# Prompt attention's value products for two heads at a time, with the linear states' load behind that stage

## What is computed

```python
s = q @ k.T - slope * dist            # 8 heads: 2 groups g of 4 heads r, head size 64
p = softmax(where(dist >= 0, s, -inf))
o_branch = p @ v                      # branch 1: selected, branch 2: window
o_a = gate[0] * o_cmp + gate[1] * o_slc + gate[2] * o_win
```

## Time and profile before

| | |
|---|---|
| median of 3 runs | 2163.66 us (2163.35 to 2164.55) |
| profiled execution | 2164.54 us, its span in the trace 2162.8 us |
| TensorE, VectorE, ScalarE, GpSimd busy | 2110.7, 1173.1, 517.1, 648.7 us |
| attention stage of the prompt, first layer | about 306 to 459 us of the span |
| granted TensorE clock, mean | 0.992 of full |

### The profile page before, as it was taken

How to read it: one execution, slowest core, us unless ns; L and a number is a source line. 1 busy time by engine, 2 the same in 40 slices (tenths; PEclk the granted TensorE clock), 3 DMA queues, 4 the chain that set the end, 5 groups by cost and what they waited for, 6 DMA issues and landing times.

```text
span 2162.8 us, 30298 instructions
## 1 busy us (share of the span) xinstructions
PE 2110.7 (98%) x11911; PEld 1689.1 (78%) x11911; DVE 1173.1 (54%) x2384; ACT 517.1 (24%) x1108; POOL 648.7 (30%) x617
## 2 busy tenths in 40 slices
PE   8998989999999999999999989899999999999999
PEld 7787866678888888888887867666788888888887
DVE  5566667855346555453336666687554364555522
ACT  3124124542112222210112231244321222222000
POOL 4240041103323444434331300421132234444332
PEclk9999999999999999999999999999999999999999
DMA  5874541112222222322283736211132222223222
GB/s 149 273 238 173 217 152 40 40 42 100 78 82 78 78 78 79 98 74 79 67 289 118 267 133 252 80 40 40 42 120 82 78 78 78 78 81 95 79 71 75
DMA packets 172303, 237.52 MB, mean 110 GB/s; under 512 B 39551, under 2 KB 151680, under 8 KB 169408
## 3 DMA queue, kind: packets, MB, share of 16 engines
q1 hardware_dynamic: 153320, 133.11, 20.4%
q0 software_dynamic: 18400, 102.36, 12.8%
q10 hardware_dynamic: 444, 0.12, 0.0%
HBM read 222.76 MB, written 21.11 MB: 113 GB/s over the span
## 4 chain that ended last, share of the span: by engine, by line
PE 91%; DVE 4%; ACT 2%; DMA 2%; issue 1%; POOL 0%; DVEq 0%; SPq 0%; ACTq 0%; POOLq 0%
PE PS L981 52%; PE PS L924 10%; PE PS L1139 6%; PE PS L946 5%; PE PS L972 3%; PE PS L1474 2%; PE PS L1391 2%; PE PS L460 2%; PE PS L1402 2%; DMA arena<-in_cache_kv_slc_dram,idx 2%; ACT arena L1685 1%; PE PS L1349 1%; DVE arena L2398 1%; PE PS L1374 1%; PE PS L1523 1%
## 5 line engine op out<-in xcount | busy, mean ns | idle before, releaser
L981 PE MATMUL PS<-arena,ring 128*128 128x272 f32 x1632 | 401.3, 393 | 0.9 <-DVE xT L2051 0.6
L981 PEld LDWEIGHTS PS<-arena,ring 128*128 128x128 f32 x1632 | 309.3, 190 | 66.0 <-issue 2.4
L1685 ACT ACTIVATE arena<-PS 128x272 f32<-128x272 f32 (+12 forms) x442 | 176.5, 423 | 723.7 <-PE PS L981 286.0
L2051 DVE TENSOR_TENSOR arena<-PS,arena 128x272 f32<-128x272 f32 (+4 forms) x298 | 138.7, 476 | 353.4 <-PE PS L981 263.4
L981 PE MATMUL PS<-hT,ring 128*128 128x272 f32 x1120 | 283.4, 398 | 5.9 <-DVE arena L2051 4.8
L981 PEld LDWEIGHTS PS<-hT,ring 128*128 128x128 f32 x1120 | 214.2, 193 | 53.6 <-DVE arena L2051 5.2
L2051 DVE TENSOR_TENSOR xT<-PS,xT 128x272 f32<-128x272 f32 x224 | 98.9, 442 | 252.2 <-PE PS L981 252.0
L840 POOL TENSOR_TENSOR qT<-ring 128x512 f32<-128x512 f32 (+1 forms) x38 | 48.8, 1285 | 385.5 <-PE PS L981 255.4
L2057 DVE SCALAR_TENSOR_TENSOR arena<-arena,prm 128x32 f32<-128x32 f32 (+1 forms) x176 | 144.1, 819 | 22.2 <-ACT arena L1685 18.2
L924 PE MATMUL PS<-hT,ring 128*128 128x272 f32 x640 | 153.9, 401 | 0.8 <-DVE small L2521 0.8
L981 PE MATMUL PS<-arena,kv_kT 128*128 128x272 f32 x616 | 149.7, 392 | 0.0
(11 more groups left out here) (361 smaller groups left out, 2975.1 us busy)
## 6 DMA issues: line engine op xcount, KB each, us to landing
ring<-in_w_up_dram SPq DMA_DIRECT2D x88, 512.0 KB, 4.6
ring<-in_w_in_dram SPq DMA_DIRECT2D x68, 512.0 KB, 4.8
ring<-in_w_down_dram SPq DMA_DIRECT2D x32, 512.0 KB, 4.4
arena<-in_state_kv_win_dram POOLq DMA_DIRECT2D x4, 2048.0 KB, 9.0
ring<-in_w_out_dram SPq DMA_DIRECT2D x16, 512.0 KB, 4.5
out_dram<-in_state_kv_win_dram POOLq DMA_DIRECT2D x2, 4064.0 KB, 39.7
ring<-in_w_down_dram SPq DMA_DIRECT2D x16, 384.0 KB, 3.5
ring<-in_w_in_dram SPq DMA_DIRECT2D x16, 256.0 KB, 4.6
```

The source lines that it names most:

```text
L981: mm = pe.matmul(PS[:, bank, 0:HALF], weight[:, k, :], rhs(k), start=(start and k == 0), stop=(stop and k == kc - 1), skip_group_check=not ...
L1685: return nc.scalar.activation(out, in_, func, **kw)
L2051: return nc.vector.tensor_tensor(out, a, b_, op)
```

## The change

Units are taken in another order: for a query tile, heads 0 and 1 with branch 1, then heads 0 and 1 with branch 2, then heads 2 and 3. Two successive units 2p and 2p+1 then have the same keys and values. Their probabilities go side by side into one buffer PTp[p % 2] of two units (key tile, unit, query), and values(p) makes one product of 256 moving columns for each key tile and group, on every even step, ahead of that step's filler. pv counts pairs. block_values moves to the first even step behind. The second buffer of PTp takes the place of S0, so GpSimd's load of S0 moves behind all the SIDED weight sums and waits for the last pv.

```diff
@@ -366,7 +366,7 @@
         kcp = sb("kcp", 32)
         vcp = sb("vcp", P)
         ex = [carve(1024 * i, 2, SEQ) for i in range(3)] + [carve(6144, 2, SEQ)]
-        PTp = [carve(3072 + 1024 * i, 2, SEQ) for i in range(2)]
+        PTp = [carve(off, 2, QT, 2, P) for off in (3072, 19136)]
 
         rT = carve(10048, GH, NT)
         xrows = xT[:, :, :].rearrange("p k n -> p (k n)")
@@ -450,15 +450,16 @@
             b = S.banks(act, f"on{h}")
             run(two(rsg[h]), pair2(b), ACT.Sqrt, bias=eps_c, scale=float(D_MODEL // DV)).then_inc(*S.drain(act, f"on{h}"))
 
-        def values(pe, units, j):
-
-            qt, r, br = units[j]
-            for g in range(G):
-                pe.wait_ge(*S.drained(pe, f"e{j}{g}"))
+        def values(pe, units, p):
+
+            qt, r, br = units[2 * p]
+            for j in (2 * p, 2 * p + 1):
+                for g in range(G):
+                    pe.wait_ge(*S.drained(pe, f"e{j}{g}"))
             for t in range(qt + 1):
                 for g in range(G):
-                    mm = pe.matmul(PS[HD * g:HD * g + HD, VBANKS[qt % 2], P * r:P * r + P], kv[:, t, 1 + br, P + HD * g:P + HD * g + HD],
-                                   PTp[j % 2][:, g, P * t:P * t + P], start=False, stop=(r == R - 1 and br == 1 and t == qt))
+                    mm = pe.matmul(PS[HD * g:HD * g + HD, VBANKS[qt % 2], P * r:P * r + 2 * P], kv[:, t, 1 + br, P + HD * g:P + HD * g + HD],
+                                   PTp[p % 2][:, g, t, :, :].rearrange("p u n -> p (u n)"), start=False, stop=(r + 1 == R - 1 and br == 1 and t == qt))
             mm.then_inc(*S.inc(pe, "pv"))
 
         def w_slot_free(eng, name):
@@ -825,8 +826,6 @@
 
                 gp.wait_ge(*S.at(gp, "arena_gla"))
                 gp.nop().then_inc(*S.inc(gp, "settled"))
-                for b in range(NB):
-                    gp.dma_start(S0[:, b, :, :], ins["state_gla"][one, b].rearrange("o (a c) k v -> (o c k) a v", c=2)).then_inc(*S.inc(gp, "s0_in", 16))
                 def weight_sums(name):
 
                     n, s = SEVEN_AT[name], wslot(name)[0]
@@ -857,6 +856,10 @@
                 gp.tensor_tensor(low[:, :, HALF:NT], high[:, :, HALF:NT], low[:, :, HALF:NT], ALU.subtract).then_inc(*S.inc(gp, "g_sum"))
                 for name in SIDED[1:]:
                     weight_sums(name)
+                gp.wait_ge(*S.at(gp, "pv"))
+                gp.nop().then_inc(*S.inc(gp, "settled"))
+                for b in range(NB):
+                    gp.dma_start(S0[:, b, :, :], ins["state_gla"][one, b].rearrange("o (a c) k v -> (o c k) a v", c=2)).then_inc(*S.inc(gp, "s0_in", 16))
                 gp.wait_ge(*S.at(gp, "gla_states", 1))
                 gp.nop().then_inc(*S.inc(gp, "settled"))
                 gp.dma_start(o_gla_p[one].rearrange("o q (a c) k v -> (o q c k) a v", c=2), states[:, 8, :, :]).then_inc(*S.inc(gp, "state_stored", 16))
@@ -1381,7 +1384,7 @@
                         mm = pe.matmul(PS[bb:bb + 32, b, 0:P], ptn[0:NS, bb:bb + 32], kv[0:NS, 4, 1, P:2 * P], start=False, stop=True)
                     mm.then_inc(*S.fill(pe, f"os{hf}"))
 
-                units = [(qt, r, br) for qt in range(QT) for r in range(R) for br in range(2)]
+                units = [(qt, r, br) for qt in range(QT) for r0 in (0, 2) for br in range(2) for r in (r0, r0 + 1)]
 
                 def score(j):
                     qt, r, br = units[j]
@@ -1438,13 +1441,14 @@
                     if j + 3 < len(units):
                         score(j + 3)
                     turn(j)
-                    if (j - 1) % (2 * R) == 0:
-                        block_values((j - 1) // (2 * R))
-                    values(pe, units, j - 1)
+                    if j % 2 == 0:
+                        if (j - 2) % (2 * R) == 0:
+                            block_values((j - 2) // (2 * R))
+                        values(pe, units, j // 2 - 1)
                     side(("u", j), "S")
                     if j in GATE_UP_AT:
                         gate_up(GATE_UP_AT[j])
-                values(pe, units, len(units) - 1)
+                values(pe, units, len(units) // 2 - 1)
                 pe.wait_ge(*S.at(pe, "kd_ready", 1))
                 pe.wait_ge(*S.claim(pe, "S", "kd"))
                 b = S.banks(pe, "kd")
@@ -1906,12 +1910,12 @@
                         exps(done)
                         done += 1
                     w = P * (qt + 1)
-                    if j >= 2:
-                        act.wait_ge(*S.at(act, "pv", j - 1))
+                    if j >= 4:
+                        act.wait_ge(*S.at(act, "pv", j // 2 - 1))
                     for g in range(G):
                         act.wait_ge(*S.filled(act, f"e{j}{g}"))
                         b = S.banks(act, f"e{j}{g}")
-                        run(PTp[j % 2][:, g, 0:w], PS[:, b, 0:w], ACT.Copy).then_inc(*S.drain(act, f"e{j}{g}"))
+                        run(PTp[j // 2 % 2][:, g, 0:qt + 1, j % 2, :], PS[:, b, 0:w].rearrange("p (t n) -> p t n", n=P), ACT.Copy).then_inc(*S.drain(act, f"e{j}{g}"))
                     decay_step(DECAY_EXP_AT.get(j))
 
 
@@ -2581,7 +2585,7 @@
 
                 def attended(qt):
 
-                    dv.wait_ge(*S.at(dv, "pv", 2 * R * (qt + 1)))
+                    dv.wait_ge(*S.at(dv, "pv", R * (qt + 1)))
                     copy(AT[:, :, P * qt:P * qt + P], PS[:, VBANKS[qt % 2], :].rearrange("p (r n) -> p r n", r=R)).then_inc(*S.inc(dv, "at_out"))
 
                 def decay_step(step):
```

## The result

The kernel after takes 2175.70 us (median of 4 runs, 2174.38 to 2176.45), the one before 2163.51 beside it (4 runs, 2162.60 to 2164.55): ratio 1.0056, 95% interval 1.0038 to 1.0073. The forecast was 2165.6, in a range to 2169.0: the direction (slower, by some 2 us) was right, and the size was missed by 10 us. The profiled execution took 2174.38 us, its span is 2172.6 (before 2162.8), TensorE busy for 2113.2 us (before 2110.7).

What follows compares the result with a forecast made beforehand. TensorE, busy for 98% of the span, was taken as the bound. First layer -0.3 + 1.5 and second -0.3 + 1.0 gave +1.9 us on the median of 2163.66: 2165.6 us, range 2158.5 to 2169.0.

Steps and rivals of the forecast that it cites:

- Part 1: Attention stage without its first three steps: merged value products gain 2.6 us a layer, 0.3 after returned waits.
- steps 3, 7, 12, 29 and 31: Attention-loop steps where TensorE loses part of the merging gain: 0.37, 0.2, 0.16, 0.4 and 1.0 us a layer.
- The lower bound of the gain: Merged value products, before returned waits: at least 2.4 us a layer, around an expected 2.6.
- Part 2: GpSimd's S0 load, eight issues of 5.86 us, moves behind the last values product: costs nothing.
- Part 3: GpSimd's earlier sums lock VectorE in weigh(0) and weigh(1), delaying turn(0) and first filler: 1.5 us lost first layer, 1.0 second.
- Rival A: VectorE's first instructions get through before GpSimd's sums, turn(0) stays: up to -2.4 us a layer, 2158.8 to 2162; chance 0.22.
- ends near 324.9 instead of 323.4: 1.5 us lost: First filler's end in the first layer's attention stage, with TensorE's full clock back at 321.7: 1.5 us later.
- rival B: Half clock around the first units lasts one step longer: +1.7 us in one or both layers, 2167.3 to 2169.0; chance 0.18.

Runs made afterwards that it cites:

- The hold: Kernel after with one more wait: GpSimd holds its first sum until VectorE has finished weigh(0) and weigh(1); 2156.89 us, 0.9976 of before.
- The hold until weigh(2): Kernel after with block_values back in step 1 and GpSimd's sums held until weigh(2) is done; 2166.87 us, 1.0018 of before.
- the second repetition of the kernel after: Kernel after, unchanged, run again beside three other kernels on one chip; 2172.52 us, 1.0039 of before.
- the split: Kernel after with one group of the side product between the second and third of the four sampled updates; 2170.77 us, 1.0034 of before.
- the delay experiment: Kernel after with the eight transposes of kd done three times, ahead of the mixers; 2186.05 us, 1.0043 of before.

## Why the prediction failed, point by point

- **Part 1.** Right in its terms: 0.43 us a merged tile, waits of 0.22, 0.22, 0.35, 0.40 and 0.89 us at steps 3, 7, 12, 29 and 31 (forecast 0.37, 0.2, 0.16, 0.4 and, with the group's saving, 1.0). The stage behind its first steps gained 1.15 us a layer instead of 0.3. By group, from the second layer, with full clock there in both profiles: values 2.6 us less, waits 2.1 more, and 0.65 less on turns and fillers, which follow one another closer where no value product stands between them (with one key tile, turn to filler 0.28 instead of 0.37 us). That last term the sum lacks, and it is most of the difference between 0.3 and 1.15. (The lower bound of the gain was mis-added: 16 x 0.15 + 40 x 0.44 = 20.0, so 2.2 and not 2.4.)
- **Part 2.** Right: eight issues in 5.86 us behind the last product, no wait at the reader. Beside VectorE's copies and memsets an issue took 0.72 to 0.83 us and landed within 2.6 to 3.4 us; ahead of the sums, before, it took 0.72 to 0.84 and landed within 2.6 to 4.8. So no stretching of the issues is seen.
- **Part 3, the mechanism.** Right: VectorE came second, turn(0) was 3.3 us late (forecast 4.5), turn(2) 0.26 (0.6), the first filler started 2.6 us later (2.95). Rival A fell: the margin was 0.1 us. What the lock does was drawn too wide: the two tensor_scalars of weigh(0) waited out one sum together (2.79 us), not one each, and the reciprocal at 304.02 took 0.15 us inside the sum of 303.90; so turn(0) was less late than forecast. The hold makes rival A true, and there the filler ended 3.0 us earlier than before (A had 0.4 to 2.1) and the kernel took 2156.89 us (A had 2158.8 to 2162). The hold until weigh(2) shows the same lock at weigh(3) and weigh(4).
- **The step that failed first**: "ends near 324.9 instead of 323.4: 1.5 us lost", which took the return of the clock at its old time. It came 3.4 us later, in five of the six layers of the three profiles of this kernel. That is rival B, which I gave 0.18, with 2.8 and 2.6 us lost in place of 1.5 and 1.0. Its "against" counted TensorE as full from 318.2 on. But the products on 31 rows, once in the hole, now came right ahead of the filler: when the half clock had lasted 10.2 us, at 319.1, the filler had run for 1.1 us (318.00). The clock did come back after 10.2 us where the filler had run longer by then: it came back at 320.7 with the filler running since 317.51 with block values in step 1, and at 319.9 with the filler running since 317.42 in the second repetition of the kernel after (first and second row below). Over all profiles with turn(0) as late as here, the half clock lasts 13.7 us in 13 of 16 layers with block values behind turn(2), and 10.2 in all six with them in step 1. The place of block values is so shown to be the cause of the longer half clock; how the clock comes to last longer, no row shows.

```profile
317.51 1.73 PE L984 MATMUL PS<-hT,ring 128*128 128x272 f32 x3
...
317.42 3.77 PE L984 MATMUL PS<-hT,ring 128*128 128x272 f32 x10
```

- **The step that failed by more**: the sum has no term for the clock anywhere else. The places that the forecast does treat, at their measured sizes, make 3.1 us (2.8 + 2.6 - 2 x 1.15) of the 11.0; the other 7.9 us are half clock at step 12 and at the updates, of whose instructions the change touches none. I had walked the stream for waits only, at full clock. Both places already stood in the trace of before, a hole of 2.38 us and some 3.8 us of matmuls on 32 rows, and neither was priced.
- **What stays open.** Removing either the hole of step 12 or the unbroken run of updates gives back 4 to 5 us, and both 9; but putting block values back gives about as much or more without touching them. Step 12 has half clock in 10 of 22 layers with its hole of 2.73 us, in 1 of 6 with the hole of 2.38, and in none of 8 without the hole. Among twelve profiles with the updates in a row seven have half clock there in some layer, of six with the split none; so much is shown. Why the kernel after has it (three profiles of three, though not in each layer), and the kernel before and the one with block values alone put back have not (one profile each), stays open: a shift of the stream against the changes of the clock is the guess that I hold, and the delay experiment does not show it. The long hole of step 12 is 2.73 us in executions with and without it.

## What to carry over

When an early product is moved by one step, ask which hole it filled: two holes close together were harmless while 2 us of small products lay between, and cost about 11 us without them, with what followed. A transfer that keeps an engine busy can be what keeps its next work out of the way of another; when it is moved, give that work an explicit wait on what must come first, and no more (one step longer cost 10 us). In a sum for a kernel at 98% of TensorE, list the places with a hole like that of step 12 (2.4 to 2.7 us) or a long run on few rows, and let the range hold a possible half clock of 2 to 3 us for each: such a place has it in some executions and in others not.

## What the runs showed of the hardware

- TensorE fell to 1.2 GHz with no idle time: from 493.2 to 496.6 it was busy for 3.40 of 3.40 us, with matmuls on 32 rows, and 0.50 followed for 6.8 us. The Trainium skill (TensorE: Matmul & The Clock Gate, Part 1) ties the level to how busy the engine was and the fall to idle time; by this row idle time is not the only ground. With eight records on 128 rows between the run's halves it never came (six profiles); with the run whole it came in seven profiles of twelve.
- The times of one kernel can fall into two groups: with the hold, six at 2154.4 to 2157.1 and four at 2161.1 to 2163.9 us. Only one of these ten has a profile, so what parts the groups is not shown. The three profiles of the kernel after have their half clock in different places, so a few single times say nothing about differences of 4 us.
- A 2-column VectorE instruction took 2.41 us where a GpSimd sum had started 0.11 us earlier, and 0.16 where it came first. A reciprocal on 2 columns took 0.15 us inside such a sum.
